# Rotary scores of two heads issued side by side, one in each row half of TensorE's array

## What the kernel computes

```python
def mla_attention(q_nope, q_rope, k_nope, k_rope, v, mask):
    s = (jnp.einsum('bqhd,bkhd->bhqk', q_nope, k_nope)
         + jnp.einsum('bqhd,bkd->bhqk', q_rope, k_rope)).astype(jnp.float32) * MLA_SCALE
    if mask is not None:
        s = jnp.where(mask[None, None], s, NEG)
    p = jax.nn.softmax(s, axis=-1)
    return jnp.einsum('bhqk,bkhd->bqhd', p.astype(v.dtype), v)
# prompt: 8 query tiles of 128 rows; key_chunk <= q_chunk in chunks of 64; 4 heads
```

## Time and profile before

| | |
|---|---|
| Time of the runs, median | 1200.02 us (3 runs, 1199.9 to 1202.46) |
| Profiled execution, span from the first to the last instruction | 1198.2 us |
| What lies around the span (median less span) | 1.8 us |
| TensorE matmul busy | 1155.7 us, 96% |
| VectorE busy | 626.0 us, 52% |
| ScalarE busy | 441.9 us, 37% |
| GpSimd busy | 71.8 us, 6% |
| Chain that ended last | TensorE 88%, VectorE 6%, ScalarE 4% |
| Mean granted TensorE clock | 0.994 |

### The profile page before, as it was taken

How to read it: one execution, slowest core, us unless ns; L and a number is a source line. 1 busy time by engine, 2 the same in 40 slices (tenths; PEclk the granted TensorE clock), 3 DMA queues, 4 the chain that set the end, 5 groups by cost and what they waited for, 6 DMA issues and landing times.

```text
span 1198.2 us, 17926 instructions
## 1 busy us (share of the span) xinstructions
PE 1155.7 (96%) x7230; PEld 1037.8 (87%) x7230; DVE 626.0 (52%) x1073; ACT 441.9 (37%) x781; POOL 71.8 (6%) x49
## 2 busy tenths in 40 slices
PE   4899999999999999999999999999999999999996
PEld 3689999999996667689999999999999757769996
DVE  4852333336448876663385233243554887766135
ACT  3552321222246544451265223122223845445122
POOL 2200001000000000002130000100000000000311
PEclk9899999999999999999999999999999999999998
DMA  9621120111123443283131211111103261107003
GB/s 332 247 75 35 35 71 17 43 52 43 49 82 135 157 142 115 71 288 144 47 114 38 75 35 35 51 36 36 57 10 105 85 218 50 45 10 255 1 28 132
DMA packets 71869, 107.70 MB, mean 90 GB/s; under 512 B 3953, under 2 KB 59377, under 8 KB 70513
## 3 DMA queue, kind: packets, MB, share of 16 engines
q1 hardware_dynamic: 71792, 106.67, 26.5%
HBM read 93.91 MB, written 11.70 MB: 88 GB/s over the span
## 4 chain that ended last, share of the span: by engine, by line
PE 88%; DVE 6%; ACT 4%; DMA 1%; issue 1%; SPq 0%; POOLq 0%; POOL 0%; DVEq 0%; ACTq 0%
PE psum L926 56%; PE psum L1299 6%; PE psum L1354 5%; PE psum L1333 3%; PE psum L1368 1%; PE psum L917 1%; DVE h_lo L1845 1%; ACT rot L1507 1%; PE psum L1289 1%; DVE w_lo L1959 1%; PE psum L1350 1%; DMA x<-in_xT 1%; PE psum L1252 1%; PE psum L1288 1%; PE psum L1137 1%; PE psum L1309 1%
## 5 line engine op out<-in xcount | busy, mean ns | idle before, releaser
L926 PE MATMUL psum<-h_hi,w_hi 128*128 128x384 f32 x1392 | 473.8, 340 | 11.3 <-DVE h_lo L1903 5.6
L926 PE MATMUL psum<-h_lo,w_hi 128*128 128x384 f32 x1392 | 465.8, 335 | 0.0
L926 PE MATMUL psum<-h_hi,w_lo 128*128 128x384 f32 x1392 | 465.7, 335 | 0.0
L926 PEld LDWEIGHTS psum<-h_hi,w_hi 128*128 128x128 f32 x1392 | 261.7, 188 | 19.6 <-issue 9.2
L926 PEld LDWEIGHTS psum<-h_hi,w_lo 128*128 128x128 f32 x1392 | 262.0, 188 | 0.5 <-issue 0.5
L926 PEld LDWEIGHTS psum<-h_lo,w_hi 128*128 128x128 f32 x1392 | 261.7, 188 | 0.0
L1959 DVE TENSOR_TENSOR w_lo<-raw,w_hi 128x1024 fp32r<-128x1024 f32 x61 | 77.3, 1267 | 202.4 <-ACT w_hi L1502 201.7
L1502 ACT ACTIVATE w_hi<-raw 128x1024 fp32r<-128x1024 f32 (+1 forms) x62 | 65.3, 1053 | 250.1 <-PE psum L926 170.3
L1354 PE MATMUL psum<-pT,ckv 128*128 128x512 f32 x144 | 74.0, 596 | 0.0
L1567 ACT ACTIVATE probs_p<-psum,nmax 128x128 f32<-128x128 f32 (+1 forms) x72 | 25.1, 361 | 120.8 <-DVE esink L1959 120.8
L761 POOL TENSOR_TENSOR sq_a<-sq_a,sq_a 128x768 f32<-128x768 f32 x12 | 22.1, 1841 | 752.2 <-ACT sq_a L1445 752.2
(11 more groups left out here) (240 smaller groups left out, 1474.9 us busy)
## 6 DMA issues: line engine op xcount, KB each, us to landing
raw<-in_w_in SPq DMA_DIRECT2D x18, 1024.0 KB, 5.4
raw<-in_w_mod SPq DMA_DIRECT2D x15, 1024.0 KB, 5.1
modw<-in_w_mod SPq DMA_DIRECT2D x8, 1024.0 KB, 14.2
raw<-in_w_out SPq DMA_DIRECT2D x10, 768.0 KB, 5.2
tab<-in_c_rope SPq DMA_DIRECT2D x6, 1152.0 KB, 5.2
x<-in_xT SPq DMA_DIRECT2D x3, 1536.0 KB, 10.0
x<-in_xT SPq DMA_DIRECT2D x2, 2304.0 KB, 10.7
x<-x_scratch SPq DMA_DIRECT2D x2, 2304.0 KB, 10.6
```

What stands on the lines that cost most here:

```text
L926: mm = pe.matmul(psum[:, bank, 0:BLK], w_[:, k, :], h[:, k, blk(n)], start=(k == 0 and i == 0), stop=(k == KD - 1 and i == 2))
```

## The change

For the first three query tiles the rotary matmul of an even head is no longer issued in its own `scores` step. The step of the even head issues the latent matmul alone and returns. The step of the odd head issues its own latent matmul and then both rotary matmuls, the even head's (array rows 0 to 63, bank of job j - 1) and the odd head's (rows 64 to 127, bank of job j), and each of the two counts up `score`. The numbers of matmuls, bytes and semaphore counts stay as they are.

```diff
@@ -1283,10 +1283,14 @@
                     if g["kind"] == "mla_p":
                         w = (t + 1) * P
                         if t < SPLIT_FROM:
-                            half = HALVES[i % 2]
                             latent_queries(1)
                             pe.matmul(out[:, 0:w], qa[:, i, tile(t)], ckvT[:, 0:w], start=True, stop=False)
-                            mm = pe.matmul(out[:, 0:w], qr[half, i // 2, tile(t)], krT[half, 0:w], start=False, stop=True)
+                            if i % 2 == 0:
+                                return
+                            for a, half in enumerate(HALVES):
+                                pe.matmul(psum[:, banks_of(j - 1 + a)[0], 0:w], qr[half, i // 2, tile(t)], krT[half, 0:w],
+                                          start=False, stop=True).then_inc(score.sem, 1)
+                            return
                         elif i == 0:
                             pe.wait_ge(key_lo.sem, key_lo.at(lane.layer, 2))
                             pe.wait_ge(q_st.sem, q_st.at(lane.layer, t - SPLIT_FROM + 1))
```

## The result

The kernel after takes 1202.53 us (median of 20 runs, 1200.93 to 1203.69), the one before beside it 1200.03 (20 runs, 1199.54 to 1202.46): ratio 1.0016, 95% interval 1.001 to 1.0022. The forecast was 1200.9 with a range of 1199.3 to 1203.2. The time lies in that range and the mechanism is the one forecast; but the loss of 2.5 us is nearly three times the +0.9 of the walk, and the rest of this text is about where the difference lies. One fact is needed to read the number: the 20 runs form two sets, ten of 1200.93 to 1201.89 at a mean clock of 0.993 and ten of 1203.17 to 1203.69 at 0.989 or 0.990. The profiled run (1203.66, span 1201.7) is of the second set. A later profile of the same kernel (`a2_again`, 1202.09, span 1199.8) has the clock at full speed in both stages, so the walk is compared with it.

The account below looks back on a forecast made before the run. VectorE was taken as all but full, with TensorE little ahead; TensorE's 4.8 us saved per layer would vanish in waits, and late signals add +0.38 and +0.49, +0.9 in sum: 1200.9 us, range 1199.3 to 1203.2.

Parts of the forecast that it names:

- the walk: Follows VectorE's delays from maxima 0 to modT 2's addition: stage later by +0.38 and +0.49 per layer, +0.9 us.
- TensorE's saving, 4.8 us per layer: Paired rotary matmuls on TensorE cost what one did: 2.08 + 1.24 + 1.46 us saved per layer.
- The rival of halves taking turns: Paired rotary matmuls on TensorE do not overlap: +3.0 us, 1203.0; chance 0.13.
- transfers of about 0.1: Assumed transfer times in the delays along VectorE, about 0.1 each; given 0.5 us per layer in the range.
- The clock is at full speed: TensorE's clock in both profiled stretches is 1.00, the 2.4 GHz level: nothing to gain or lose.
- new waits at four places: TensorE waits ahead of latent 10 and 11 (about 1.2 each), job 10 (ScalarE) and for the modulation row.
- The saving lands: TensorE's 4.8 us per layer come through whole, -9.6: 1190.4; chance 0.06 in part or whole.
- 2.2 us per layer at most: VectorE's idle pieces cap the gain even with no late signal: -4.4 us in all, 1195.6.

Follow-up runs that it names:

- e7: Pairs only for jobs 4 to 9, and the start of all three written step orders changed, against the kernel before: 1196.02 us, ratio 0.9963.
- e4: Pairs only for jobs 4 to 9, the other jobs as in the kernel before, against that kernel: 1199.25 us, ratio 0.9991.
- e6: Kernel after plus two full float32 128x320 matmuls at four places per layer's stage; against the kernel before: 1202.02 us, ratio 1.0009.

## Why the prediction came out as it did

- **TensorE's saving, 4.8 us per layer, a pair at the price of one: right.** 0.92 for 0.91 and 0.70 for 0.70; the first two pairs took 2.05 off by latent 8 (L1252 at 372.58 for 374.63), where 2.08 were forecast. The Trainium skill ("TensorEngine Tiling (Array Packing)", Key Properties), by which different tiles run in parallel, is borne out for this shape. The rival of halves taking turns is out: its job 1 pair would have ended 0.64 later, and maxima 0 was forecast at 368.40 and came at 368.38.
- **The walk along VectorE: right in every place, a little short in size.** Forecast and `a2_again`: maxima 1 370.81 and 370.84; modulation row 388.36 and 388.45; L1403 388.93 and 389.02; maxima 10 391.95 and 392.16; L1372 403.06 and 403.32. The waits of TensorE stand where they were forecast; those ahead of latent 10 and 11, forecast at about 1.2 each, read 1.00 and 0.81. The first layer ends its step +0.66 instead of +0.38, the second +0.72 instead of +0.49. Of the 0.26 in the first, 0.09 arose by the copy of the modulation row, 0.07 where TensorE starts again after a wait (L1403 lasts 0.58, where without a wait it lasted 0.51), 0.05 between the end of job 11's pair and maxima 10 (I had put 0.10 there; it took 0.14, and the rows before already had 0.15, from 391.78 to 391.93), and 0.06 between maxima 10 and the second modulation row. I had put transfers of about 0.1 together and gave them 0.5 per layer in the range; they all went one way. In the whole: +1.4 instead of +0.9, and 0.2 behind the stages, which I have not located.
- **"The clock is at full speed (1.00, the 2.4 GHz level) in both stretches, so nothing is to be had or lost there": wrong, and the larger part of the error.** The row told of a TensorE that stood still for 0.69 us at most there. The walk itself took that away: it forecast new waits at four places, which eat up what TensorE saved, and no term of the sum asked what they do to the clock. Going by the times and the mean clocks, it then fell in about half of the runs; one such run is profiled. In the profile with the fall the second stage is 52.67 us long instead of 51.39, 1.28 more; a further 0.4 or so comes from the short fall at 71.6 us, ahead of the stage (it begins at 352.43 instead of 352.00). Together that is the distance of the two sets, 1.7. The expectation should have been a mixture of +1.6 and +3.3, and the median of 20 lies between them.
- **That the time fell into the range owes something to luck.** The forecast's own range was 1199.6 to 1202.2; the ten runs of the quicker set lie in it, the median of 1202.53 does not. It is covered only because the range was widened to 1203.2 for the halves taking turns, a rival that is out; and by the time alone that rival (1203.0) would be nearer than the forecast. What bears the forecast out is the timeline, not the time.
- **The saving lands: out**, but its cause is now exact. The saving of jobs 4 to 9 can land, by 0.8 as the lists stood and by 1.6 to 1.7 in lists that bring 0.25 themselves. Of the first two pairs nothing does, since maxima 0 stands at the head of VectorE's list with everything behind it ready. I had said that VectorE could give back 2.2 us per layer at most; e7 comes near with 1.9.
- **The Trainium skill's rule that tiling does not speed up the evacuation of PSUM** ("TensorEngine Tiling (Array Packing)", PSUM Bottleneck) was a right warning; the trace agrees in that TensorE waits 1.17 for ScalarE and 1.04 for VectorE at job 10 and L1403. But these waits come of a late first result and a fixed order more than of the rate at which PSUM is read: with the same reads, e4 brings 0.82 per layer and e7 1.9.

## What to carry to other kernels

Two results that become ready together are one result that is late: before matmuls are paired, look who waits for the first of the two and what is queued behind it, and pair only where that queue is somewhere else at the time. A saving on one engine wants new lists for all of them, or part of it turns into waits (0.8 landed with the old lists, 1.9 with the new). And a new wait of TensorE may have a second price beside its length: when a change gives TensorE slack in a stage with a full clock, look whether that clock falls in some of the runs, as it very likely did here.

## What the runs showed of the hardware

- Two float32 matmuls on the two row halves of the array run wholly side by side: four records in 0.92 us at 384 columns, 0.70 at 256, and 0.49 at 128 (0.91, 0.70 and 0.48 for one, in the kernel before).
- Eight full matmuls of 320 columns, put where TensorE waited, cost nothing in the stage's length (e6 +0.63 and +0.68, `a2_again` +0.66 and +0.72).
- When an even head's latent matmul is followed directly by a product into another bank, the product's first record starts 0.03 us behind the start of the latent matmul's second pass and lasts 0.64 instead of 0.33, so the two lie over each other in the trace; starts and ends keep the program's order, and the next product follows 0.48 later, so nothing is gained by it (the kernel after, first layer; the latent matmul began at 365.20):

```profile
365.59 0.49 PE L1287 MATMUL psum<-ckvT,qa 128*128 128x384 f32 x1
365.62 0.64 PE L1252 MATMUL psum<-cq_hi,mq_hi 128*128 128x384 f32 x1
366.10 0.33 PE L1252 MATMUL psum<-cq_hi,mq_lo 128*128 128x384 f32 x1
```

- In the stretch with the lower clock a product of 384 columns takes 0.52 us and follows the last by 0.32, against 0.34 and 0.17; yet the 6.8 us of it cost the stage only 1.28, since it took up 1.5 us of waits (1.16 ahead of job 10, and 0.38 of the 1.13 at L1403).
